# Seven short products in front of long ones: one at the fourth input tile of five stage entries, one at each gate's sixth tile

## The reference, cut to what matters

```
for i in range(2):
    h = rms_norm(x, g_pre_mix[i])
    if i == 0: mix = short_conv_mixer(h, ...)
    else:      k, v = shared_kv(x, g_kv, w_kv); mix = diff_attention(h, k, v, ...)
    x = x + rms_norm(mix, g_post_mix[i])
    ffn = conv_ffn(rms_norm(x, g_pre_ffn[i]), w_ffn_up[i], w_ffn_conv[i], w_ffn_down[i])
    x = x + rms_norm(ffn, g_post_ffn[i])
    gate = sigmoid(rms_norm(x, g_pre_ple[i]) @ w_ple_gate[i])
    x = x + rms_norm(gate * (p[i] @ w_ple_proj[i]), g_post_ple[i])
```

## Time and profile before

| what | value |
|---|---|
| median of 3 runs | 1229.33 us |
| lowest, highest | 1225.73, 1229.62 us |
| profiled execution | 1228.74 us |
| its span, first to last instruction | 1226.9 us |
| mean granted TensorE clock | 0.993 |
| matmuls | 10122 |

### The profile page before, as it was taken

How to read it: one execution, slowest core, us unless ns; L and a number is a source line. 1 busy time by engine, 2 the same in 40 slices (tenths; PEclk the granted TensorE clock), 3 DMA queues, 4 the chain that set the end, 5 groups by cost and what they waited for, 6 DMA issues and landing times.

```text
span 1226.9 us, 24212 instructions
## 1 busy us (share of the span) xinstructions
PE 1203.0 (98%) x10122; PEld 1179.0 (96%) x10122; DVE 883.4 (72%) x1464; ACT 734.2 (60%) x1258; POOL 18.6 (2%) x36
## 2 busy tenths in 40 slices
PE   9999999999999999999999999999999999999997
PEld 8999799999999999999999999999899899999997
DVE  6886566764547777444876899856787877999565
ACT  6873456664446666344655666655766876666555
POOL 1120000000000000000000000000000000000000
PEclk9999999999999999999999999999899999999998
DMA  7233144655552666654664666474374236664741
GB/s 275 84 120 100 56 163 145 209 176 186 174 171 88 205 210 197 196 190 146 207 203 139 190 208 211 156 229 154 123 239 157 92 123 198 210 209 164 227 139 35
DMA packets 59753, 205.51 MB, mean 167 GB/s; under 512 B 6739, under 2 KB 9340, under 8 KB 59516
## 3 DMA queue, kind: packets, MB, share of 16 engines
q1 hardware_dynamic: 57536, 201.21, 50.3%
q10 hardware_dynamic: 2108, 2.75, 0.7%
HBM read 202.87 MB, written 1.06 MB: 166 GB/s over the span
## 4 chain that ended last, share of the span: by engine, by line
PE 85%; ACT 6%; DVE 6%; DMA 1%; issue 1%; ACTq 0%; DVEq 0%
PE PS L380 68%; PE PS L424 2%; PE PS L428 2%; PE PS L425 2%; PE PS L392 2%; DVE WL L363 2%; ACT WH L356 1%; DMA RAW<-wpack 1%; PE PS L476 1%; PE PS L2506 1%; PE PS L534 1%; ACT EE L2664 1%; ACT L546 1%; DMA X<-xin 1%; PE PS L711 0%
## 5 line engine op out<-in xcount | busy, mean ns | idle before, releaser
L363 DVE TENSOR_TENSOR WL<-RAW,WH 128x1024 fp32r<-128x1024 f32 (+2 forms) x387 | 459.1, 1201 | 207.3 <-ACT WH L356 206.8
L356 ACT ACTIVATE WH<-RAW 128x1024 fp32r<-128x1024 f32 (+2 forms) x387 | 392.8, 1035 | 205.6 <-PE PS L380 177.0
L380 PE MATMUL PS<-UH,WH 128*128 128x256 f32 (+1 forms) x1464 | 412.4, 282 | 5.7 <-DVE WL L363 3.1
L380 PE MATMUL PS<-UH,WL 128*128 128x256 f32 (+1 forms) x1464 | 409.0, 279 | 0.0
L380 PE MATMUL PS<-UL,WH 128*128 128x256 f32 (+1 forms) x1464 | 408.8, 279 | 0.0
L380 PEld LDWEIGHTS PS<-UH,WH 128*128 128x128 f32 x1464 | 274.8, 188 | 7.1 <-issue 3.5
L380 PEld LDWEIGHTS PS<-UL,WH 128*128 128x128 f32 x1464 | 275.3, 188 | 0.0
L380 PEld LDWEIGHTS PS<-UH,WL 128*128 128x128 f32 x1464 | 274.8, 188 | 0.0
L380 PE MATMUL PS<-HH,WL 128*128 128x272 f32 (+1 forms) x512 | 144.4, 282 | 0.0
L380 PE MATMUL PS<-HH,WH 128*128 128x272 f32 (+1 forms) x512 | 144.4, 282 | 0.0
L380 PE MATMUL PS<-HL,WH 128*128 128x272 f32 (+1 forms) x512 | 144.2, 282 | 0.0
(11 more groups left out here) (421 smaller groups left out, 2011.5 us busy)
## 6 DMA issues: line engine op xcount, KB each, us to landing
RAW<-wpack SPq DMA_DIRECT2D x361, 512.0 KB, 4.1
RAW<-wpack SPq DMA_DIRECT2D x18, 384.0 KB, 3.6
RAW<-wpack SPq DMA_DIRECT2D x6, 256.0 KB, 2.7
C<-cst SPq DMA_DIRECT2D x1, 1072.0 KB, 6.1
HB<-bias_rows ACTq DMA_DIRECT2D x1, 1024.0 KB, 5.2
out<-X SPq DMA_DIRECT2D x4, 256.0 KB, 2.3
X<-xin SPq DMA_DIRECT2D x2, 272.0 KB, 5.7
X<-xin ACTq DMA_DIRECT2D x2, 272.0 KB, 5.7
```

What stands on the lines that cost most here:

```text
L356: a.e.activation(WH[n % NH][:, 0:w], RAW[n % NR][:, 0:w], ACT.Copy).then_inc(*a.mark("wh", n))
L363: v.e.tensor_tensor(WL[n % NH][:, 0:w], RAW[n % NR][:, 0:w], WH[n % NH][:, 0:w].bitcast(f32), ALU.subtract).then_inc(*v.mark("wl", n))
L380: ins = t.e.matmul(o, part(n, hw, kw, a, b), x(kx), start=first and not i and not p, stop=last and i == len(kcs) - 1 and p == 2)
```

## The change

`first_products` gets an argument `spare`, a bank; at input tile k == 3 it issues one matmul of 192 columns into that bank, with the weights and the input of the first product of that tile. Nobody reads it. Five calls pass it: ffn0, ffn1, gate0, gate1 and kv. A new function `spare_bank` takes the next bank and puts the counter back, so the order of banks stays as it was. It is evaluated as an argument of the call. And the gates' output tile (u, m) == (2, 1), the sixth of eight, gets `short=192`.

```
+        def spare_bank(t, st):
+
+            n = banks.n
+            b = banks.take(t, ("spare", st), None)
+            banks.n = n
+            return b
+
-        def first_products(t, bs, xh, xl, ready, w):
+        def first_products(t, bs, xh, xl, ready, w, spare=None):
 
             for _, n in bs:
                 t.wait_ge("wl", n)
             for k in range(8):
                 t.wait_ge("uh", *ready(k)[1:])
+                if k == 3 and spare is not None:
+                    t.e.matmul(PS[:, spare, 0:192], part(bs[0][1], 1, k, 0, 128), xh(k)[:, 0:192], start=True, stop=True)
...
-                    first_products(t, bs, uh, ul, u_ready, S).then_inc(*t.mark("ffn", layer, 1, 1))
+                    first_products(t, bs, uh, ul, u_ready, S, spare_bank(t, st)).then_inc(*t.mark("ffn", layer, 1, 1))
...
-                    first_products(t, bs, uh, ul, g_ready, S).then_inc(*t.mark("gate", layer, 1, 1))
+                    first_products(t, bs, uh, ul, g_ready, S, spare_bank(t, st)).then_inc(*t.mark("gate", layer, 1, 1))
...
-                        products(t, PS[:, b, 0:S], n + m, pairs[0:4], 0, 128, uh, ul, g_ready, True, False)
+                        products(t, PS[:, b, 0:S], n + m, pairs[0:4], 0, 128, uh, ul, g_ready, True, False,
+                                 short=192 if (u, m) == (2, 1) else 0)
...
-            first_products(t, bs, uh, ul, u_ready, S).then_inc(*t.mark("dif", "k", 3))
+            first_products(t, bs, uh, ul, u_ready, S, spare_bank(t, "kv")).then_inc(*t.mark("dif", "k", 3))
```

## The result

| | before | after |
|---|---|---|
| median | 1228.66 us (6 runs, 1225.03 to 1230.59) | 1236.04 us (6 runs, 1233.71 to 1238.95) |
| profiled execution: span, time | 1226.9, 1228.74 | 1231.9, 1233.71 |

The ratio is 1.0065, with a 95% interval of 1.0052 to 1.0078: 8.0 us slower, 6.4 to 9.6. (The medians are 7.4 us apart, the means of the six, 1228.05 and 1236.03, 8.0.) The forecast was 5.2 us slower. The time stands inside the range, the sign is right, and the size is short by 2.8 us.

The account below looks back on a forecast made before the run. TensorE bounds the kernel: matmuls busy 98% of the span, chain 85% on PE. 2 x 1.45 (ffn) + 2 x 1.1 (gates) + 0.11 (kv) - 0.05 (gate1's sixth tile) = 5.2 us, giving 1234.5 us; range 1230.5 to 1237.

Parts of the forecast that it names:

- The bank's wait: At ffn and gate entries PE waits for ACT's embed copy: 1.45 us per ffn, 1.1 per gate, short products included.
- the low half's stall: At tile 0 of the four entries the wait for the low half goes; in gates 0.27 us with its restart.
- carried whole: Behind the entries: no slack found, so each entry's delay shifts all that follows and counts in full.
- Rival B: Entry bank waits carried nowhere or already over; only short products count, 1229.1 to 1230.1 us; chance 0.10.
- the root sums: Behind each of the four entries the root sum was to come 1.0 to 1.5 us later.
- The late start: First matmul 1.29 us late in each ffn entry, 1.57 in each gate, with 0.14 from ACT's copy to matmul.
- The short products: At five entries and the gates' sixth tile, each costs 0.113 us and leaves a good pace as it is.
- the turn: A short product may turn the bad pace good, gaining 4.4 ns per matmul behind it: 0.27 us in an entry.
- gate1's sixth tile: Short product before gate1's sixth output tile: between -0.21 and +0.11 us, taken as -0.05.
- C: Low-clock stretch near 879.5 to 886 missing from the median execution after: 3.3 us less, 1231.2 us; chance 0.15.
- D: Added idle of 1.3 to 1.6 us at an entry makes the clock fall there: 1237.8 us; chance 0.07.
- The ten microseconds from 636: Stretch before ffn0 with as much idle time and the clock at 1.00, taken as speaking against the clock falling.

Follow-up runs that it names:

- Experiments 1: The change with the spare bank taken at input tile 3, all seven short products kept, against the kernel before: 1228.96 us, ratio 1.001.
- experiment 2: Bank taken in front of the entries as in the change, no short product issued, against the kernel before: 1234.27 us, ratio 1.0058.
- Experiment 5: All of the change, with the bank's wait moved behind the entry's waits for weights and high half: 1238.05 us in its single execution.
- experiment 7: Only the short product at each gate's sixth output tile, nothing at the entries, against the kernel before: 1228.97 us, ratio 1.001.
- experiment 3: No short products; the ffn and gate entries wait for the next pair's embed copy, against the kernel before: 1251.04 us, ratio 1.0184.
- experiment 4: Kernel before plus waits for the next pair's embed copy at ffn and gate entries, 26 unread matmuls before each: 1238.82 us, ratio 1.0092.

## Why the prediction was right, and where its size was off

**The bank's wait: right, and shown.** Its place (four entries, none at kv, where PE's idle time in front is 0.09 us), its releaser (the first copy of the pair), the idle times (1.4 to 1.7 us for 1.3 and 1.6), the low half's stall that goes, and that it is carried whole were as stated. Experiments 1 and 2 separate it from the short products: 7.1 of 8.0 us with it alone, 1.2 without it. Rival B, no loss, is refuted by the result and by experiment 2. Read against the copies, the root sums come 2.2 us (ffn0), 1.2 (gate0), 1.9 (ffn1) and 1.6 (gate1) later, where I had 1.0 to 1.5; the next two points say why.

**The late start: mis-sized, the main term.** I had 0.14 us from the end of ACT's copy to the matmul, read where one wait stood in front of it, and so 2 x 1.29 + 2 x 1.57 = 5.7 us for the four. Measured: 6.7. The 1.0 us is PE's further waits, which now queue behind the blocked one. In the trace, the records of PE's own sequencer show the blocked wait in ffn0 as one of 3.12 us, from 660.22 to 663.34 (the copy ends at 663.29), and further semaphore instructions behind it: at 663.39, 663.59 and 663.69 in ffn0, at 852.51 and 852.62 in gate0. They are left out of the timeline's rows. Before, the waits for the weights had been worked off while earlier matmuls ran (660.39 to 660.60 in ffn0). Experiment 5 takes them from behind the blocked wait, and the 0.14 us returns in all four entries.

**The short products: each costs about 0.11 us as reckoned, but the turn was too hopeful.** The tile with the short product takes 0.10 to 0.11 us longer than its neighbours in all five entries (in ffn1 1011.74 - 1010.24 = 1.50 for 1.42, the pace having turned within it). At ffn0, kv and gate1 the pace was bad and stayed so. Against what stood in the sum: ffn0 96 x 4.4 ns = 0.42 us for 0.05, kv 0.4 for nothing, gate1 0.3 for a turn that did not come, ffn1 0.1; gate0 gives 0.1 back, being good from the start, and gate1's sixth tile (below) 0.15. Together 0.9 us in the profiled execution. Behind gate1's sixth tile the chain has 72 matmuls at 114.0 ns, so there it turned:

```profile
1210.36 8.21 PE PS L380 x72
```

With both, 5.2 becomes 7.1 us. Set against the profiled pair, from which the paces were read, 1.3 us of ffn0's long stretch and about half of C's 3.3 us come off, which leaves about 4.2 of the 5.0 measured.

The medians, however, can't be answered with one execution's paces, which differ where the instructions don't (experiment 7). Without any term for the pace the sum is 6.7 us of late starts and 0.8 for seven short products, less 0.5 for the gates' two low-half stalls: 7.0, inside the measured interval of 6.4 to 9.6. What is left to the 8.0 is not settled. It is of the size of what one long stretch at the other pace gives or takes, and I can't assign it. That the paces fell out well or badly in the one profiled execution is chance as far as these runs show.

**The clock.** C did not decide the medians, although the profiled execution shows that such a stretch can be halved. D did not come true at 1.4 to 1.7 us of idle time: behind the two longest idle stretches, in gate0 and gate1, the granted clock is 1.00 in the windows of the changed kernel, and so behind the other two.

```profile
852.70:859.50 6.80, 6.78 (x59) 6.80 (x60) 6.70 (x14) 5.85 (x12) 0.00 (x0) 1.00 0.01 2
...
1194.90:1201.00 6.10, 6.10 (x52) 6.10 (x53) 6.10 (x13) 5.16 (x11) 0.00 (x0) 1.00 0.01 3
```

It came true in experiment 3 at 3.4 us, four times in four. The 11 us between experiments 3 and 4 make 2.8 us a time, where I had 3.3. The Trainium skill (page "TensorE: Matmul & The Clock Gate", section "Why this matters for your kernels") says to leave no long idle gap of TensorE between bursts of matmuls, or its clock goes back to the low level. Experiment 3 agrees, with the clock at 0.50 behind 3.3 to 3.7 us of idle time, and experiment 4, where the gap is filled, too. The ten microseconds from 636, which the prediction set against that rule, held 1.5 us of idle time in all and so were no case of it.

## What to carry to other kernels

A helper that hands out a buffer may also emit a wait: look at where it is called, not at where the buffer is used, and ask what stands behind that wait on an in-order queue. Here a matmul of 0.11 us cost over 1.6 us, because its bank was taken three tiles of work too early, and one moved line gives nearly all of it back. When a wait becomes the late one, put it last: the waits behind it are each paid after it is released.

## What the runs showed of the hardware that was not expected

Waits that are already satisfied are not free once they queue behind one that blocks: about 0.1 us each (0.31 us to the first matmul with two behind it, 0.42 and 0.51 with three, 0.14 with none).

At one granted clock the same stream of 256-column matmuls runs at 113.3 or 117.8 ns, keeps its pace for hundreds of matmuls, and can have either at the same place in two kernels whose code up to there is the same (gate0's entry, before and in experiment 7). A matmul of 192 columns in the stream can turn the slower pace into the faster one: at seven of fourteen entries, and at the gates' sixth tile, where the faster pace followed it at ten of ten places and at four of ten without it. It never did the reverse, in five entries. What sets the pace was not found.
